# One decoder layer on one core: the router of each token tile inside the next tile's output projection, the sample tile kept by halves on 128 partitions, the router's logits in four column strips

## The chip, the core and the metric

The kernel runs on one core of a Trainium2 chip. The metric is the device time of one execution in microseconds (us). A smaller number is better.

## What is computed

One layer of a hybrid decoder for 256 prompt tokens and 64 sample tokens (8 sequences of 8), all in fp32. Attention, a gated linear recurrence and their merge come first; none of that is touched. What follows is this:

```python
h = x + merged @ w_o                                   # (320, 1024) @ (1024, 1024)
x2 = rmsnorm(h, norm2)
logits = x2 @ w_router + b_router                      # 32 experts
top_v, top_e = lax.top_k(logits, 4); gate = softmax(top_v)
# every expert: its tokens, in slots
u = x @ w1[e] + b1[e]                                  # (1024 -> 2048), glu and lin interleaved
y = (min(glu,7) * sigmoid(1.702*glu) * (clip(lin)+1)) @ w2[e] + b2[e]
out = h + sum over the 4 experts of gate * y
```

The weights of the 32 experts are 12 MB each (8 for w1, 4 for w2), 384 MB together, and each is read once.

## The kernel before, in words

The tokens are three tiles (`TILES`): 128 and 128 prompt tokens, and 64 sample tokens. Each engine has its program written out by hand, and semaphores tie them together; there is no planner, so the order of the work is the order of the calls in each engine's block.

**The weight stream.** Expert weights pass through `ring`, 19 slots of 1 MB. `CHUNKS` (L88) is their order: w1 of an expert in 8 chunks, w2 in 4, with the w2 of an expert after the w1 of the next in part. The SP queue issues chunks 0 to 6 once two state outputs have left, 7 and 8 in the first branch projection, 9 to 14 when the merge is done, and 15 to 18 when the output projection of all three tiles is done (`sp.wait_ge(h_psum, 3)`, L388), because they go where `w_o` lay. From chunk 19 on, each waits until the chunk that had its slot 19 places earlier has been used (`await_used`, L372).

**The stage around the change.** TensorE (PE) runs this list, L850 to L866:

```python
project_h(0); project_h(1); turn_h(0); project_h(2); turn_h(1)
logits(0); turn_h(2); logits(1); logits(2)
for t in range(3): places(t)
```

`project_h` (L799) is one tile's output projection: 32 matmuls of 128x512 in two column halves for a prompt tile (L810), and for the sample tile 32 of 64x512 whose halves run side by side on column tiles (L815). `turn_h` (L819) transposes h, 8 times 128x128. `logits` (L831) multiplies the transposed h by the router's weights, 8 steps of k into one 32-column result. `places` (L841) counts with triangular and all-one matrices which slot a token has at each expert. An fp32 matmul of the code is two instructions in the trace. VectorE (DVE) does `add_h` (h = x + projection, L1576), `turned_h` (copies the transposed h out of PSUM and multiplies by norm2, L1588), `rms_h` (L1596), then `choose` for the three tiles (L1603: bias, top 8, indices, one-hot, sum, the last two being L1608 to L1618), one `placed` (L1639), and `pick_tokens` (L1673), six compares that build the 0/1 matrices `pick` of the first two experts. ScalarE (ACT) does `squares_h` and `root_h` (L1213, L1220): the sum of squares, the root, and `hn`, the normed h. The sample tile lies on partitions 0 to 63 with all 1024 columns.

Then the experts run in pairs, `body(p)` (L983). `gather` (L880) multiplies `pick` by `hn`, six matmuls of 512 columns (L886, 12 instructions), of which two have 64 rows; ACT copies the result (L1268), PE transposes it (L895), DVE multiplies it by norm2. `up` (L899, L914) is w1 of an expert, 64 instructions, `down` (L951) is w2, 32; L928 turns u; `combine` (L968) adds y to `acc` with DVE's `add` (L1726). The gather of the next pair is the last work of each body; only the first stands before the bodies. `last_body` (L1017) has another order: its second `up` waits for DVE's adds of the pair before. At the end `store_tile` (L419) writes the three tiles of `acc`.

## Time and profile before

| what | value |
|---|---|
| median of 3 runs | 1259.48 us (1259.46 to 1260.38) |
| the profiled execution, its own time | 1260.13 us |
| its span in the trace | 1258.3 us |
| busy: PE, DVE, ACT | 1204.7, 346.0, 185.8 us |
| moved by DMA | 439.83 MB, mean 350 GB/s |
| mean granted clock of TensorE | 0.991 |

The profiled execution took 0.65 us more than the median; the span lacks 1.8 us of it, before the first and after the last record. "PE" rows are matmuls, "PEld" rows weight loads, "SPq" the issue of transfers. In a row of the timeline, the second number is the time from the start of the group to its end, and a bracket says how long the engine was idle before it and what ended that. In a row of the windows, the numbers are the stretch, its length, and the busy time of PE, PEld, DVE, ACT and POOL with their instructions, then the granted clock (1 is full), the DMA share and GB/s. Matmuls overlap, so the distance between the starts of two groups tells more than the length of one.

### The profile page before, as it was taken

The page shows a single profiled execution, that of the slowest core. Times are in us where ns is not written, and L with a number is a line of the kernel's source. Part 1 is how long each engine was busy: PE and PEld are TensorE (multiplying, and loading weights), DVE is VectorE, ACT ScalarE, POOL GpSimd, SP SyncE. Part 2 cuts the span into 40 slices and gives each one's busy share as a digit, 9 for nine tenths or more (in the row PEclk, how much of TensorE's full clock was granted, in tenths as well). Part 3 has the DMA queues.
Part 4 walks back from the last instruction along what each step waited for, and adds up shares of the span by engine and source line. Part 5 has one row for each costly group of instructions (what it writes and reads, how often), then busy time and mean ns, then how long its engine had stood idle before and what let it go on. Part 6 is the DMA issues. An engine that isn't in the chain of part 4 may idle for free.

```text
span 1258.3 us, 12744 instructions
## 1 busy us (share of the span) xinstructions
PE 1204.7 (96%) x5349; PEld 542.6 (43%) x5349; DVE 346.0 (27%) x727; ACT 185.8 (15%) x330; POOL 24.9 (2%) x49
## 2 busy tenths in 40 slices
PE   5999999998999999999999999999999999999987
PEld 4776678744333434343333434333333333333332
DVE  2405423614232222223132222321221313131222
ACT  2115321003111111111011111111010101010111
POOL 4101000000000000000000000000000000000000
PEclk9999998998999999999999999999999999999999
DMA  9833153943999999999999999999999999999995
GB/s 242 261 114 120 34 134 119 393 203 134 375 381 418 417 417 417 418 418 416 417 418 416 417 419 416 416 418 417 417 418 417 416 417 417 417 417 417 417 416 213
DMA packets 101484, 439.83 MB, mean 350 GB/s; under 512 B 15822, under 2 KB 31536, under 8 KB 68608
## 3 DMA queue, kind: packets, MB, share of 16 engines
q1 hardware_dynamic: 99632, 434.88, 86.8%
q0 software_dynamic: 1776, 4.09, 1.1%
q8 instruction: 44, 0.72, 0.2%
q14 instruction: 16, 0.13, 0.0%
q10 hardware_dynamic: 16, 0.00, 0.0%
HBM read 436.26 MB, written 3.67 MB: 350 GB/s over the span
## 4 chain that ended last, share of the span: by engine, by line
PE 74%; DMA 17%; SPq 4%; ACT 2%; DVE 1%; issue 1%; DVEq 0%; ACTq 0%
PE ps L914 25%; DMA ring<-in_w 17%; PE ps L951 13%; PE ps L581 10%; PE ps L886 7%; PE ps L968 5%; PE ps L783 3%; PE ps L810 2%; SPq L370 2%; SPq L368 2%; PE ps L928 1%; PE ps L559 1%; PE ps L895 1%; ACT xnT L1258 1%; DMA acc<-in_x_sample 1%
## 5 line engine op out<-in xcount | busy, mean ns | idle before, releaser
L914 PE MATMUL ps<-ring,hnT 128*64 128x512 f32 x2048 | 451.8, 595 | 14.7 <-DMA ring<-in_w 11.3
L914 PEld LDWEIGHTS ps<-ring,hnT 128*64 128x64 f32 x2048 | 155.4, 137 | 298.3 <-issue 262.4
L951 PE MATMUL ps<-ring,xnT 128*64 128x512 f32 x1024 | 230.6, 598 | 5.0 <-DMA ring<-in_w 3.6
L951 PEld LDWEIGHTS ps<-ring,xnT 128*64 128x64 f32 x1024 | 78.0, 138 | 150.8 <-issue 130.5
L1708 DVE TENSOR_TENSOR xnT<-ps,b1T 128x512 f32<-128x512 f32 x32 | 22.1, 692 | 415.8 <-PE ps L928 415.8
L581 PE MATMUL ps<-xnT,ring 128*128 128x320 f32 x464 | 130.3, 436 | 0.6 <-DVE xnT L1343 0.6
L1729 DVE TENSOR_TENSOR acc<-acc,ps 128x1024 f32<-128x1024 f32 x34 | 41.4, 1218 | 235.6 <-PE ps L968 235.6
L1245 ACT COPY hnT<-ps 128x1024 f32<-128x1024 f32 x32 | 32.4, 1012 | 481.1 <-PE ps L914 481.1
L581 PEld LDWEIGHTS ps<-xnT,ring 128*128 128x128 f32 x464 | 86.5, 190 | 37.8 <-issue 2.2
L886 PE MATMUL ps<-region,cst 128*128 128x512 f32 (+1 forms) x192 | 97.7, 635 | 1.6 <-DVE cst L1678 1.6
L968 PE MATMUL ps<-xnT,cst 128*128 128x512 f32 (+1 forms) x192 | 79.1, 617 | 4.2 <-ACT xnT L1258 2.7
L886 PEld LDWEIGHTS ps<-region,cst 128*128 128x128 f32 (+1 forms) x192 | 31.6, 190 | 55.7 <-issue 54.6
L1257 ACT COPY xnT<-ps 64x512 f32<-64x512 f32 x32 | 18.5, 579 | 239.9 <-PE ps L951 239.9
L968 PEld LDWEIGHTS ps<-xnT,cst 128*128 128x128 f32 (+1 forms) x192 | 25.0, 171 | 48.4 <-issue 42.1
L928 PEld LDWEIGHTS ps<-cst,hnT 128*128 128x128 f32 x256 | 33.2, 209 | 28.3 <-issue 23.5
L928 PE MATMUL ps<-cst,hnT 128*128 128x128 f32 x256 | 39.2, 296 | 2.8 <-ACT hnT L1245 2.8
L1700 DVE TENSOR_TENSOR hnT<-ps,cols 128x512 f32<-128x512 f32 x32 | 21.9, 692 | 58.7 <-PE ps L895 58.6
L1268 ACT COPY hnT<-ps 128x512 f32<-128x512 f32 x32 | 18.7, 585 | 69.0 <-PE ps L886 69.0
L810 PE MATMUL ps<-ring,xnT 128*128 128x512 f32 x64 | 27.7, 593 | 1.2 <-issue 1.2
L1251 ACT ACTIVATE sig<-xnT 128x512 f32<-128x512 f32 x32 | 20.2, 630 | 27.4 <-DVE xnT L1712 27.4
L1688 DVE TENSOR_SCALAR cst<-cst,place,gates 128x64 f32<-128x64 f32 (+1 forms) x96 | 22.6, 303 | 0.0
L1719 DVE SCALAR_TENSOR_TENSOR hnT<-hnT,xnT 128x512 f32<-128x512 f32 x32 | 22.2, 693 | 1.1
(255 smaller groups left out, 668.5 us busy)
## 6 DMA issues: line engine op xcount, KB each, us to landing
ring<-in_w SPq DMA_DIRECT2D x384, 1024.0 KB, 22.1
ring<-in_w_in SPq DMA_DIRECT2D x15, 1024.0 KB, 5.7
ring<-in_w_o SPq DMA_DIRECT2D x1, 4096.0 KB, 16.3
acc<-in_x_prompt SPq DMA_DIRECT2D x4, 512.0 KB, 9.4
ring<-in_w_in SPq DMA_DIRECT2D x8, 256.0 KB, 5.8
ring<-in_w_a SPq DMA_DIRECT2D x2, 1024.0 KB, 10.2
ring<-in_w_b SPq DMA_DIRECT2D x1, 2048.0 KB, 15.4
out<-ring POOLq DMA_DIRECT2D x1, 1024.0 KB, 7.9
```

The source lines that it names most:

```text
L368: sp.dma_start(ring[:, m, :], w1v[e, k]).then_inc(chunk_in[m], 16)
L370: sp.dma_start(ring[:, m, :].rearrange("p (f c) -> p f c", f=2), w2v[e, k]).then_inc(chunk_in[m], 16)
L581: mm = pe.matmul(ps[:, bank, 0:T], unit(m)[:, k, c:c + P], xnT[:, k, :], start=(k == 0), stop=(k == KD - 1))
L783: mm = pe.matmul(ps[:, u % 3, 0:T], w_sb[:, k, P * m:P * m + P], operand[:, k, :], start=(k == 0), stop=(k == 3))
L810: mm = pe.matmul(ps[:, (XB, VB_)[t] + c, :], xnT[:, k, t0:t0 + r], wo_sb[:, k, 512 * c:512 * c + 512], start=(k == 0), stop=(k == KD - 1))
L886: mm = pe.matmul(ps[:, XB + half, :], pick[0:r, t, :], hn[0:r, t, 512 * half:512 * half + 512], start=(t == 0), stop=(t == 2))
L914: mm = pe.matmul(ps[o:o + 64, q // 2, :], xeT[:, k, SLOTS * which:SLOTS * (which + 1)], ring[:, slot, 512 * q:512 * q + 512], start=(k == ...
L928: mm = pe.transpose(ps[:, 2 + gl, o:o + P], u_sb[:, q, 256 * r + gl:256 * r + gl + 255:2], ident)
L951: mm = pe.matmul(ps[64 * c:64 * c + 64, 6, :], hT[:, which, order_of(f), :], ring[:, slot, D * (f % 2) + 512 * c:D * (f % 2) + 512 * c + 512],
L968: mm = pe.matmul(out, lhsT, rhs[:, 512 * half:512 * half + 512], start=True, stop=True)
L1245: nc.scalar.copy(u_sb[:, :, :], ps[:, 0:2, :]).then_inc(u_copied, 1)
L1729: dve.tensor_tensor(acc[:, t, :], acc[:, t, :], ps[:, bank:bank + 2, :].rearrange("p a b -> p (a b)"), ALU.add).then_inc(comb_added, 1)
```

## The change

Three things. (1) PE's list is cut up: the second half of tile 1's projection and all of tile 2's are issued in pieces, and between the pieces stand the transposes, logits and places of the tile before. DVE and ACT are put in the same order, tile by tile, and each tile's `pick` for the first two experts is made as soon as its places are known, so that the first gather's parts for tiles 0 and 1 run before tile 2's choice. (2) Logits come in four column strips: the router's weights, scaled once by norm2 on DVE, become the 32-column stationary operand, four k at a time side by side, two steps; ACT copies the 128-partition result, and one matmul with a constant `fold` adds the strips and turns the result. (3) The sample tile lies by halves on 128 partitions: columns 0 to 511 on partitions 0 to 63, columns 512 to 1023 on 64 to 127, in `acc`, `hn`, loads, stores and adds. Its sum of squares is joined over the two halves by a matmul with the constant `twin`, its transposes are four, and the 64-row matmuls of every gather lie on different row halves, next to each other. `pick_tokens` is three instead of six operations. The constants grow by 224 columns.

```diff
@@ constants
-                  ("chunk_of", 4), ("seq_of", 8), ("head_of", 4), ("keep", 320), ("slot", 128),
-                  ("expert", 32)]:
+                  ("chunk_of", 4), ("seq_of", 8), ("head_of", 4), ("keep", 320), ("slot", 64),
+                  ("expert", 32), ("twin", 128), ("before_s", 128), ("fold", 32)]:
@@ SP: loads and stores of the sample tile
+            for half in range(2):
+                sp.dma_start(acc[64 * half:64 * half + 64, 2, 0:512], x_half(x_sample, half)
+                             ).then_inc(x_again[2], 16)
...
+                    for half in range(2):
+                        sp.dma_start(x_half(y_sample, half), acc[64 * half:64 * half + 64, 2, 0:512]).then_inc(y_out, 16)
@@ PE: new functions
+            def logit_parts(t):
+                t0, r = TILES[t]
+                pe.wait_ge(hnT_ready, t + 1)
...
+                for step in range(2):
+                    for a in range(4):
+                        k = 4 * step + a
+                        mm = pe.matmul(ps[32 * a:32 * a + 32, 2, 0:r], w_rt[:, k, :], hnT[:, k, t0:t0 + r],
+                                       start=(step == 0), stop=(step == 1))
+                mm.then_inc(lgp_psum, 1)
+
+            def logits(t):
+                pe.wait_ge(lgp_copied, t + 1)
...
+                pe.matmul(ps[:, 0, 0:EXPERTS], lg_parts, const("fold"), start=True, stop=True).then_inc(lg_psum, 1)
...
+            def twin_sum():
+                pe.wait_ge(ss2_ready, 3)
+                pe.wait_ge(placed_freed, 1)
+                pe.matmul(ps[:, NB, 128:129], const("twin"), small[:, 46:47], start=True, stop=True).then_inc(twin_psum, 1)
+
+            def pick_part(half, t, start, stop):
+                if t < 2:
+                    return pe.matmul(ps[:, XB + half, :], pick[:, t, :], hn[:, t, 512 * half:512 * half + 512],
+                                     start=start, stop=stop, skip_group_check=True)
+                return pe.matmul(ps[:, XB + half, :], pick[64 * half:64 * half + 64, 2, :],
+                                 hn[64 * half:64 * half + 64, 2, 0:512], start=start, stop=stop, skip_group_check=True)
+
+            def first_part(half, t):
+                pe.wait_ge(pick_ready, t + 1)
+                pe.wait_ge(hn_ready, t + 1)
...
+                pick_part(half, t, start=(t == 0), stop=False)
@@ PE: the order
-            project_h(0)
-            project_h(1)
+            project_h(0, 0, range(KD))
+            project_h(0, 1, range(KD), last=True)
+            project_h(1, 0, range(KD))
             turn_h(0)
-            project_h(2)
+            project_h(1, 1, range(4))
+            logit_parts(0)
+            project_h(1, 1, range(4, 6))
+            logits(0)
+            project_h(1, 1, range(6, KD), last=True)
+            pe.wait_ge(pads_ready, 6)
+            project_h(2, 0, range(2))
+            places(0, [0])
             turn_h(1)
-            logits(0)
+            project_h(2, 0, range(2, 4))
+            logit_parts(1)
+            project_h(2, 0, range(4, 5))
+            logits(1)
+            project_h(2, 0, range(5, KD), last=True)
+            places(1, [0, 1])
             turn_h(2)
-            logits(1)
+            first_part(0, 0)
+            twin_sum()
+            logit_parts(2)
+            first_part(1, 0)
             logits(2)
...
+            first_part(0, 1)
+            first_part(1, 1)
+            places(2, [0, 1])
+            places(2, [2])
+            pe.wait_ge(pick_ready, 3)
+            pe.wait_ge(hn_ready, 3)
+            for half in range(2):
+                pick_part(half, 2, start=False, stop=True).then_inc(gather_done, 1)
@@ PE: every later gather
                 for half in range(2):
-                    for t, (_, r) in enumerate(TILES):
-                        mm = pe.matmul(ps[:, XB + half, :], pick[0:r, t, :], hn[0:r, t, 512 * half:512 * half + 512],
-                                       start=(t == 0), stop=(t == 2))
-                    mm.then_inc(gather_done, 1)
+                    pick_part(half, 2, start=True, stop=False)
+                for half in range(2):
+                    pick_part(half, 0, start=False, stop=False)
+                    pick_part(half, 1, start=False, stop=True).then_inc(gather_done, 1)
@@ ACT: order
+            squares_h(0)
+            root_h(0)
+            copy_parts(0)
+            squares_h(1)
+            root_h(1)
+            copy_parts(1)
+            squares_h(2)
+            act.wait_ge(hnT_psum, 3)
+            nc.scalar.copy(hnT[:, :, PROMPT:T].rearrange("p (h k) s -> p k h s", h=2),
+                           ps[:, 0, :].rearrange("p (k h s) -> p k h s", k=4, h=2)).then_inc(hnT_ready, 1)
+            copy_parts(2)
+            root_h(2)
@@ DVE: order
             add_h(0)
+            rms_h(0)
+            dve.tensor_tensor(w_rt[:, :, :], w_rt[:, :, :], wide(cols[:, 8:16].unsqueeze(2), [P, KD, EXPERTS]), ALU.mult
+                              ).then_inc(rt_scaled, 1)
             dve.wait_ge(stores, 16 * 20)
             turned_h(0)
-            rms_h(0)
+            choose(0)
             add_h(1)
+            placed(0)
+            turned_h(1)
             rms_h(1)
+            choose(1)
             add_h(2)
-            turned_h(1)
-            turned_h(2)
+            placed(1)
             rms_h(2)
-            for t in range(3):
-                choose(t)
-            placed()
+            choose(2)
+            placed(2)
```

`placed(t)` is one operation as before plus one compare of 128x128 for `pick`; `copy_parts(t)` is ACT's copy of the strips, 128x128 (two of 128x64 for tile 2). `weigh`, which works out the gate weights after the first gather, has six operations in place of twelve. The six matmuls that count the tokens of each expert stand between the last part of the first gather and its transposes.

## Rows read from the trace of the kernel before

**Rows 1.** The page: transfer rate in 40 slices; the chain by line.
```profile
GB/s 242 261 114 120 34 134 119 393 203 134 375 381 418 417 417 417 418 418 416 417 418 416 417 419 416 416 418 417 417 418 417 416 417 417 417 417 417 417 416 213
...
PE ps L914 25%; DMA ring<-in_w 17%; PE ps L951 13%; PE ps L581 10%; PE ps L886 7%; PE ps L968 5%; PE ps L783 3%; PE ps L810 2%; SPq L370 2%; SPq L368 2%; PE ps L928 1%; PE ps L559 1%; PE ps L895 1%; ACT xnT L1258 1%; DMA acc<-in_x_sample 1%
```

**Rows 2.** Windows: busy us (x instructions) of engines, PEclk, DMA share, GB/s.
```profile
304.00:306.00 2.00, 1.44 (x2) 0.83 (x3) 0.41 (x3) 0.00 (x0) 0.00 (x0) 0.50 0.00 0
...
368.00:370.00 2.00, 2.00 (x12) 0.86 (x10) 1.19 (x7) 0.00 (x0) 0.00 (x0) 1.00 0.55 86
370.00:375.00 5.00, 5.00 (x26) 1.98 (x24) 0.00 (x0) 0.00 (x0) 0.00 (x0) 1.00 0.85 331
...
1242.00:1244.00 2.00, 2.00 (x12) 0.75 (x10) 0.00 (x0) 0.00 (x0) 0.00 (x0) 1.00 0.12 47
```

**Rows 3.** Timeline of PE in later bodies: start, us, line [idle before].
```profile
593.27 13.95 PE L914 MATMUL ps<-ring,hnT 128*64 128x512 f32 x64 [0.16 <-issue]
...
650.01 13.95 PE L914 MATMUL ps<-ring,hnT 128*64 128x512 f32 x64 [0.16 <-issue]
...
1155.41 1.94 PE L914 MATMUL ps<-ring,hnT 128*64 128x512 f32 x8 [0.22 <-DMA ring<-in_w]
```

**Rows 4.** Chain of waits, gather to first expert: start us, us, what.
```profile
304.56 7.68 PE ps L886 x12
...
312.90 0.65 PE ps L895 x4
...
313.60 13.98 PE ps L914 x64
```

**Rows 5.** Timeline of the stage, PE and the weight queue.
```profile
255.20 27.70 PE L810 MATMUL ps<-ring,xnT 128*128 128x512 f32 x64 [1.15 <-issue]
...
282.75 1.04 PE L827 MATMUL ps<-cst,acc 128*128 128x128 f32 x8
...
283.71 7.09 PE L815 MATMUL ps<-ring,xnT 128*64 128x512 f32 x32
...
291.21 24.73 SPq L370 DMA_DIRECT2D ring<-in_w  x4
```

**Rows 6.** Timeline of VectorE: first and last operation of a choice, compares.
```profile
295.06 0.25 DVE L1608 SCALAR_TENSOR_TENSOR xnT<-ps,small,b_rt 128x32 f32<-128x32 f32 x1
...
296.41 0.37 DVE L1616 TENSOR_REDUCE sel<-xnT 128x32 f32<-128x128 f32 x1
...
303.35 1.06 DVE L1678 TENSOR_SCALAR cst<-cst,place 128x64 f32<-128x64 f32 x6
```

**Rows 7.** Chain in attention: column strips, row halves, plain projection.
```profile
69.44 1.22 PE ps L573 x16
...
124.12 1.06 PE ps L619 x8
125.19 4.50 PE ps L581 x16
```

**Rows 8.** Timeline of PE's weight loads inside one body's gather.
```profile
1178.53 0.29 PEld L886 LDWEIGHTS ps<-region,cst 64*128 64x128 f32 x2 [0.76 <-issue]
1179.58 0.30 PEld L886 LDWEIGHTS ps<-region,cst 128*128 128x128 f32 x2 [0.76 <-issue]
```

**Rows 9.** Windows where the granted clock is below full.
```profile
350.00:355.00 5.00, 5.00 (x21) 1.52 (x19) 0.14 (x1) 0.00 (x0) 0.00 (x0) 0.77 1.03 428
...
294.40:297.80 3.40, 1.94 (x16) 1.86 (x16) 2.56 (x13) 2.58 (x3) 0.00 (x0) 0.99 1.00 400
...
304.60:308.00 3.40, 3.40 (x4) 1.10 (x4) 0.00 (x0) 0.00 (x0) 0.00 (x0) 0.50 0.00 0
```

**Rows 10.** Timeline of the last 50 us: tile 2's add, last matmuls, stores.
```profile
1214.24 0.69 DVE L1733 TENSOR_TENSOR acc<-acc,ps 64x512 f32<-64x512 f32 x1
...
1239.62 7.09 PE L951 MATMUL ps<-ring,xnT 128*64 128x512 f32 x32 [1.32 <-issue]
...
1251.41 3.56 SPq L422 DMA_DIRECT2D out<-acc  x3
```

271 lines of the change are left out of this document (140 added, 131 removed).

## The prediction

> **What bounds the kernel now.** I read the page first. In slices 13 to 39 of its 40 the transfers run at 416 to 419 GB/s, and the chain that ended last holds both PE lines and the weight transfer with 17% [rows 1]. So two things share the bound, and the question is where each does. A pair of experts is 24 chunks of 1.0486 MB; at 417 GB/s a chunk takes 2.51 us and a pair 60.3. PE's own period, where nothing waits for DMA, is 650.01 - 593.27 = 56.7 us [rows 3]. PE is thus faster by 3.6 us a pair, lives on the ring's 19 slots for some bodies, and then stands behind the stream: late bodies wait before single chunks [rows 3]. From there on the end is set by when the stream started, not by what PE does in the middle.
>
> When did it start? The windows show the transfers at rest before the first expert, and once more short of full between 368 and 375 us [rows 2]: there 2 x 0.45 + 5 x 0.15 = 1.7 us are missing by share, 2.6 by GB/s. This is the place that decides. The first body uses 20 chunks, 20 are loaded behind it, and the 21st place comes free only with the first chunk of the second body's first matmuls. After 375 the stream never pauses. So **the time at which the second body begins passes to the end one to one**: whatever PE saves before it is kept, whatever PE saves in the bodies after it is lost in the wait for chunks, until the last stretch, where the stream is over before PE is (its share is 0.12 in 1242 to 1244 [rows 2], while the last `down` runs to 1246.7 and the stores start at 1251.41 [rows 10]).
>
> Ahead of the second body lies the stage that the change rebuilds. PE is dense from 255.20 to 290.8: projections of tiles 0 and 1 in 27.7 us, transposes of tile 0, tile 2's projection in 7.09 [rows 5]. Then come 14 us of transposes, logits, choices and places, most of it waiting for DVE, and from 304.56 the gather, 7.68 us, and the copy and the transposes, to the first expert at 313.60 [rows 4].
>
> **Part by part, the stage.** Prices: an instruction of 128x512 takes 27.7/64 = 0.433 us, eight transposes 1.04 [rows 5]. Four column strips appear in the attention part: 16 instructions of 320 columns take 1.22 [rows 7]; by columns 128 would be 0.49, and 16 weight loads bound it below, so I take 0.6 (0.4 for 64 columns), with 0.49 and 1.22 as ends. A change of the tile shape on PE costs something: two 64-row instructions between others span 1179.58 - 1178.53 = 1.05 us, not 0.87, so 0.2 with the exposed weight load [rows 8].
>
> A rule of the Trainium skill speaks against the change here: its page "TensorEngine Tiling (Array Packing)", section "Key Properties", says that switching the tiling mode, not just the tile, drains TensorE. By the row the drain is 0.2 us, and the sum goes by that.
>
> Until tile 2's projection is done, PE gets, in front of the 290.8 of before: tile 1's transposes 1.0, two sets of strips 1.2, two folding matmuls 0.5, tile 0's places 0.25 and nine shape changes 1.8. That is 4.8, so it ends at 295.6. The choices run beside it. A choice takes 296.41 + 0.37 - 295.06 = 1.7 us on DVE up to `sel` [rows 6]; tile 0's starts near 283.5 and `sel` is there at 285.3, where PE wants it at 287.4; tile 1's transposes need DVE's add by 287.6 and get it at 286.7; tile 1's second set of strips waits for DVE's copy until 290.0, and PE comes at 290.6; tile 1's fold needs ACT's copy at 292.3 and PE comes at 292.6. All are in time, the last two by half a microsecond: if that cover goes, each late item adds its lateness. The add of tile 1 on DVE now queues behind `choose(0)`, the copy of the strips on ACT behind `root_h`; both are in these times.
>
> After 295.6: DVE's add of tile 2 0.7 (one operation of 128x512 in place of two), four transposes 0.5, the first `pick` piece 0.87, the `twin` matmul 0.25, strips with shape changes 0.8, a piece 0.87, the fold 0.25: 299.8, with 0.3 for handovers 300.1. Then the only serial piece left, tile 2's choice: `sel` 1.75 later, 301.9. In its shadow PE runs two pieces, 1.73, and the places of tiles 0 and 1, 0.5, to 302.4; the last place matmul, 302.7; DVE's `placed` and one compare, 0.3 + 0.35 (two of the compares of 1.06/6 [rows 6]) with handovers 0.1: 303.5. Four 64-row pieces remain of the gather. They lie on different row halves; eight such instructions of 256 columns took 1.06 us, where plain ones of 320 columns take 4.50/16 = 0.28 each, or 0.225 at 256 and 1.80 for eight [rows 7]. The first pass of the second half can run beside the second pass of the first: 4 become 3 steps, 1.3 us, bounded by 0.87 and 1.73. With a shape change: 305.0. Six counting matmuls 0.5 + 0.2, the eight transposes 1.06 + 0.2: **the first expert at 307.0 instead of 313.6, 6.6 us earlier.** ACT's exponentials lie between its last `hn` and the gather's copies, as before, under the choice and the places.
>
> **Clock.** The granted clock fell to 0.50, the lower level of 1.2 GHz, after 294.4 to 297.8, in which PE had 1.94 us of 32-column logits, and was still there in 304.6 to 308.0, where four gather instructions took 3.4 us [rows 9], twice their price. That loss of 1.7 us is inside the old 313.6 and not in my 307.0, which is at full clock. The new stage is denser, but 301 to 306 holds waits; I charge 0.6 for a fall there, between 0 and 3. The dip in 350 to 355 (0.77, 1.2 us lost) behind the narrow bias matmuls of the first body I take to stay.
>
> **Handovers.** The new chain has a dozen more semaphores on the edge of PE's order; I charge 0.6.
>
> **The first body.** Its gather for the next pair has 12 instructions with four shape changes, 5.2 + 0.8; the new order has 1.3 + 8 x 0.433 + two changes = 5.2: 0.8 saved, ahead of the second body, so kept. In the 13 bodies after it the same 0.8 is worth nothing (cover: the stream, 60.3 against now 55.9). If the stream were not the bound, it would be 10 us more.
>
> **The last stretch.** Gather of the last pair 0.8, and the adds of tile 2 before the last `up`, one operation less, 0.7 [rows 10]. Together 1.5, and the stream allows it: the last chunks land before 1244 and the last `down` wants its fourth near 1239.6 + 5.3 = 1244.9 [rows 2, 10]. Below nothing it can't be, above 1.5 the chunks stop it. At the very end one add less, 0.7, against one more transfer to issue; three took 3.56 us with their waits for DVE [rows 10]; I take 0.3 for it: 0.4 left.
>
> **At nothing:** 112 KB more constants, 0.3 us of transfer among the first projections (cover: PE's L581, which the chain holds there [rows 1]; without it, 0.3), the second load of x by one more issue on SP, first needed by the add at 269, chunks 15 to 18 issued 5 us later than at 291.21 [rows 5]: 10 us of transfer, done near 306, wanted in the second `up` after 321. SP has nothing else queued behind that wait but chunk 19, which waits for the first expert. `weigh`, the scaling of the router's weights and `pick_tokens` lie under PE's matmuls.
>
> **Sum:** 6.6 - 0.6 - 0.6 + 0.8 + 1.5 + 0.4 = 8.1 us off. The profiled execution took 1260.13, so 1252.0; against the median of 1259.48, 1251.4.
>
> **Rivals.**
> *A, as above:* 0.62, own range 1249.3 to 1253.5. The low side is strips at 0.49, no fall of the clock, and no dip near 350.
> *B, the clock falls under the first expert.* The stretch before it is now small matmuls, a wait for the last choice, and transposes. If the lower level, which before lay over some 10 us, from 297.8 at the earliest to 308.0 [rows 9], lies over 303 to 313, the first `up` runs at half speed in it: 6 us at half the clock do 3 us of work, and with the small things ahead of it 3.6 more are lost than A holds. For: the fall came behind just such matmuls. Against: gather pieces now stand among them. 1255.0; chance 0.17.
> *C, handovers stall PE.* The two covers of about half a microsecond fail and each of the waits behind (strips, fold, choice) is late by as much again: 2 us, 1253.6; 0.11. Against: where the old chain changes engines, from ACT's copy to 312.90 and on to 313.60, it leaves less than 0.1 us [rows 4].
> *D, the stream does not move.* If the pause at 368 to 375 were not PE's doing but the stream's own, the end would stay but for 1 us at the very end: 1258.5. For: 17% of the chain is the transfer. Against: with every slot loaded there is nothing to send, and at 304 to 306 the share is 0 [rows 2]. 0.04.
> *E, slower: the shape changes.* The old stage had PE pass 35 us without a break; the new one cuts in strips, halves and full shapes, some 16 changes to the first expert. I price each at 0.2. At 0.7 the gain is eaten, at 0.9 the kernel takes 1262.5. That is the skill's rule with a large price. The 0.18 of [rows 8] speaks against; but it was seen between 64 rows and 128 only, not between 32 columns and 128. 0.04.
> The remaining 0.02 is that the change doesn't save because the strips don't run side by side: then 3 x 1.1 us more, 1254.7, still faster.
>
> **The numbers.** A measurement here tells 0.2% or 2.5 us from nothing. Faster: A, B, C and the rest, less a little for B beyond bounds, 0.91; same: D, 0.05; slower: E, 0.04. The range has to take A whole, C, and B's middle: 1249.0 to 1255.4.
>
> **What would show it.** First L914 of the first expert (`up`) near 307 to 308 where it was 313.60; tile 2's projection ending near 296; DVE's three choices at about 283.5, 293 and 300; the strips 0.6 us a set; the last two `pick` pieces within 1.3; a gather of 5.1 in every body; the pause near 361 to 367 still there; PE's idle time before chunks larger than now by about 0.8 a body. Wrong would be: transfers without that pause, PE waits of over half a microsecond between projection pieces, or 0.50 as the clock under the first `up`.

## The result, and the profile after

The changed kernel takes 1245.79 us (median of 9 runs, 1243.53 to 1251.26); the kernel before, run beside it, 1259.46 (9 runs, 1253.59 to 1263.27). The ratio is 0.9899, with a 95% interval of 0.9879 to 0.9920: faster by 1.0%. The forecast was 1251.4, in a range of 1249.0 to 1255.4. The sign was right; the gain was 13.7 us and not 8.1, outside the range. One run of `after_third` (2457.11 us) and one of `late_bias_fill` (1551.94) further on were slow ones: the medians in the table below contain them, the ratios leave them out.

The profiled execution took 1247.42 us with a span of 1245.6, 12.7 less than before. PE is busy for 1181.6 us (1204.7 before), DVE for 327.6 (346.0), ACT for 186.0, and the mean granted clock is 0.996 (0.991). Lines of the code have moved; those of the rows below are: L823 and L828 output projection (prompt, sample tile), L841 transposes of h, L855 strips, L863 fold, L876 places, L885 `twin`, L889 and L891 gather with 128 and 64 rows, L938 counts, L968 transposes after the gather, L987 `up`, L1001 transposes of u, L1024 `down`, L1041 `combine`; on DVE L1677 the add of tile 2, L1700 to L1710 a choice, L1716 and L1719 `placed` and the compare, L1789 the multiplication by norm2.

The page of the kernel after: transfer rate in 40 slices, and the chain by line.

```profile
GB/s 263 243 81 150 44 135 39 401 281 167 417 416 417 417 416 418 417 417 416 418 417 417 418 418 417 417 417 416 418 417 416 417 417 416 417 417 417 417 417 229
...
DMA ring<-in_w 26%; PE ps L987 21%; PE ps L596 10%; PE ps L1024 9%; SPq L381 4%; PE ps L1041 4%; PE ps L889 4%; SPq L383 3%; PE ps L798 3%; PE ps L823 2%; PE ps L1001 1%; PE ps L574 1%; PE ps L891 1%; PE ps L968 1%; PE ps L715 1%
```

Against [rows 1]: full rate from the eleventh slice on, with none below it until the last, where before the eleventh and twelfth held 375 and 381. The transfer is now 26% of the chain in place of 17%.

The windows of the kernel after, where before had no transfers and then a pause [rows 2], and where its clock was down [rows 9]; columns as in front.

```profile
294.40:297.80 3.40, 3.17 (x33) 1.92 (x29) 1.35 (x5) 1.30 (x3) 0.00 (x0) 1.00 0.46 125
297.80:301.20 3.40, 3.40 (x16) 1.93 (x13) 1.65 (x9) 3.25 (x11) 0.00 (x0) 1.00 0.99 405
301.20:304.60 3.40, 2.48 (x18) 1.34 (x19) 0.48 (x2) 1.21 (x4) 0.00 (x0) 1.00 1.02 418
304.60:308.00 3.40, 3.10 (x18) 1.15 (x19) 3.25 (x11) 0.00 (x0) 0.00 (x0) 1.00 0.73 290
360.00:362.00 2.00, 2.00 (x12) 0.86 (x10) 0.00 (x0) 0.00 (x0) 0.00 (x0) 1.00 0.97 391
...
368.00:370.00 2.00, 2.00 (x12) 0.81 (x10) 0.00 (x0) 1.01 (x1) 0.00 (x0) 1.00 1.04 416
370.00:375.00 5.00, 5.00 (x26) 1.95 (x24) 0.00 (x0) 0.00 (x0) 0.00 (x0) 1.00 1.02 418
350.00:355.00 5.00, 4.76 (x18) 2.35 (x19) 2.96 (x6) 1.55 (x3) 0.00 (x0) 1.00 1.01 418
```

Two things that the prediction took for given are gone: the clock is at its full level (2.4 GHz) in every one of these stretches, and the pause of the stream behind the first body doesn't come, which the prediction had named as a sign of being wrong.

The chain of waits of the kernel after, from tile 2's first matmuls to the first expert (start us, us, what). "x4" with 0.7 us is half of eight instructions where the other half hides.

```profile
285.40 1.87 PE ps L828 x8
287.27 0.34 PE ps L876 x2
287.61 0.91 PE ps L841 x8
288.52 1.87 PE ps L828 x8
290.38 0.57 PE ps L855 x16
290.96 1.01 PE ps L828 x4
291.97 0.34 PE ps L863 x2
292.31 2.75 PE ps L828 x12
...
295.08 0.70 DVE acc L1677
...
297.45 0.36 PE ps L855 x16
...
301.55 0.20 DVE place L1716
...
301.77 0.30 DVE cst L1719
...
302.12 1.18 PE ps L891 x4
303.30 0.57 ACT hnT L1362
...
303.92 0.67 PE ps L968 x4
...
304.61 0.70 DVE hnT L1789
...
305.36 0.64 PE ps L987
```

In this execution the projection starts at 255.83 (255.20 before [rows 5]), so this list has to be read 0.63 earlier against the old one. The first expert starts at 305.36 in place of 313.60 [rows 4]: from the projection's start that is **49.53 us in place of 58.40**. No piece of the projection waits for another engine; the strips take 0.57 a set and 0.36 for tile 2, and the only waits of PE above 0.1 us are DVE's add, the last choice's end (`placed` and the compare), and behind the gather ACT's copy and DVE's multiplication.

PE's groups in the first body, before (313.60 to 366.31) and after (305.36 to 354.83); columns: count, busy us and mean ns, idle.

```profile
L951 PE MATMUL ps<-ring,xnT 128*64 128x512 f32 x32 | 8.8, 712 | 0.0
L886 PE MATMUL ps<-region,cst 128*128 128x512 f32 (+1 forms) x12 | 6.0, 626 | 0.0
```
```profile
L1024 PE MATMUL ps<-ring,xnT 128*64 128x512 f32 x32 | 7.1, 595 | 0.0
L889 PE MATMUL ps<-region,cst 128*128 128x512 f32 x8 | 3.7, 606 | 0.0
L891 PE MATMUL ps<-region,cst 64*128 64x512 f32 x4 | 1.2, 629 | 0.0
```

The first body lost 3.2 us, 52.71 to 49.47: `down` 1.7 because the fall of the clock is gone (0.77 in 350 to 355 before [rows 9], 1.00 now), the gather 1.3. And from the timeline of PE at the end of the kernel after, the last chunk's matmuls:

```profile
1226.19 5.50 PE L1024 MATMUL ps<-ring,xnT 128*64 128x512 f32 x24 [1.32 <-ACT xnT L1352]
1232.24 1.94 PE L1024 MATMUL ps<-ring,xnT 128*64 128x512 f32 x8 [0.55 <-DMA ring<-in_w]
```

The last `down` starts 13.4 us earlier than at 1239.62 [rows 10], and its fourth part then stands 0.55 us for the last chunk.

So the 12.7 us of span are: projection 0.63 later, stage 8.87 shorter, first body 3.24 shorter, all that follows the second body's start 1.2 shorter (892.0 to 890.8).

### The profile page after: what moved, and what is told of

Read it like the earlier page. It is cut to its first block, busy times and chain, and to the rows that moved or that the text cites. A ratio compares the mean times of both kernels' runs of the same rounds, so it can differ in the third digit from the quotient of the medians.

```text
span 1245.6 us, 12704 instructions
## 1 busy us (share of the span) xinstructions
PE 1181.6 (95%) x5353; PEld 529.7 (43%) x5353; DVE 327.6 (26%) x656; ACT 186.0 (15%) x335; POOL 24.9 (2%) x49
## 4 chain that ended last, share of the span: by engine, by line
PE 62%; DMA 26%; SPq 7%; ACT 2%; DVE 1%; issue 1%; DVEq 0%; ACTq 0%
DMA ring<-in_w 26%; PE ps L987 21%; PE ps L596 10%; PE ps L1024 9%; SPq L381 4%; PE ps L1041 4%; PE ps L889 4%; SPq L383 3%; PE ps L798 3%; PE ps L823 2%; PE ps L1001 1%; PE ps L574 1%; PE ps L891 1%; PE ps L968 1%; PE ps L715 1%
## 5 line engine op out<-in xcount | busy, mean ns | idle before, releaser
L987 PE MATMUL ps<-ring,hnT 128*64 128x512 f32 x2048 | 453.7, 595 | 15.6 <-DMA ring<-in_w 14.9
L987 PEld LDWEIGHTS ps<-ring,hnT 128*64 128x64 f32 x2048 | 154.4, 137 | 302.0 <-issue 253.0
L1024 PE MATMUL ps<-ring,xnT 128*64 128x512 f32 x1024 | 233.1, 596 | 16.1 <-DMA ring<-in_w 14.7
L1024 PEld LDWEIGHTS ps<-ring,xnT 128*64 128x64 f32 x1024 | 73.7, 137 | 169.1 <-issue 122.0
L596 PE MATMUL ps<-xnT,ring 128*128 128x320 f32 x464 | 134.2, 446 | 0.5 <-DVE xnT L1437 0.5
L1041 PE MATMUL ps<-xnT,cst 128*128 128x512 f32 (+1 forms) x192 | 79.1, 617 | 4.3 <-ACT xnT L1352 2.7
L889 PE MATMUL ps<-region,cst 128*128 128x512 f32 x128 | 59.6, 606 | 0.0
L1041 PEld LDWEIGHTS ps<-xnT,cst 128*128 128x128 f32 (+1 forms) x192 | 25.0, 171 | 48.5 <-issue 42.1
L1001 PEld LDWEIGHTS ps<-cst,hnT 128*128 128x128 f32 x256 | 33.1, 208 | 28.3 <-issue 23.5
L1001 PE MATMUL ps<-cst,hnT 128*128 128x128 f32 x256 | 39.2, 296 | 2.8 <-ACT hnT L1339 2.8
L889 PEld LDWEIGHTS ps<-region,cst 128*128 128x128 f32 x128 | 22.8, 189 | 33.5 <-issue 33.4
L1789 DVE TENSOR_TENSOR hnT<-ps,cols 128x512 f32<-128x512 f32 x32 | 22.0, 691 | 31.7 <-PE ps L968 29.7
L823 PE MATMUL ps<-ring,xnT 128*128 128x512 f32 x64 | 28.4, 596 | 1.2 <-issue 1.2
L1362 ACT COPY hnT<-ps 128x512 f32<-128x512 f32 x32 | 18.6, 585 | 40.4 <-PE ps L889 38.5
L968 PE MATMUL ps<-cst,hnT 128*128 128x128 f32 x128 | 20.0, 280 | 3.9 <-ACT hnT L1362 3.9
```

The costliest lines, as they stand in the source:

```text
L596: mm = pe.matmul(ps[:, bank, 0:T], unit(m)[:, k, c:c + P], xnT[:, k, :], start=(k == 0), stop=(k == KD - 1))
L823: mm = pe.matmul(ps[:, (XB, VB_)[t] + c, :], xnT[:, k, t0:t0 + r], wo_sb[:, k, 512 * c:512 * c + 512], start=(k == 0), stop=(k == KD - 1), ...
L889: return pe.matmul(ps[:, XB + half, :], pick[:, t, :], hn[:, t, 512 * half:512 * half + 512], start=start, stop=stop, skip_group_check=True)
L968: mm = pe.transpose(ps[:, bank, P * k:P * k + P], xe[:, P * (4 * half + k):P * (4 * half + k) + P], ident)
L987: mm = pe.matmul(ps[o:o + 64, q // 2, :], xeT[:, k, SLOTS * which:SLOTS * (which + 1)], ring[:, slot, 512 * q:512 * q + 512], start=(k == ...
L1001: mm = pe.transpose(ps[:, 2 + gl, o:o + P], u_sb[:, q, 256 * r + gl:256 * r + gl + 255:2], ident)
```

## The experiments

Each edit is to the kernel after, unless it says before. `fill(n)` is n matmuls of 128x512 whose result is thrown away, 2 x 0.433 us each; they are the price of PE time at a place. In the text "stage" is from the projection's start to the first `up`, "first body" from there to the next body's first `up`, "rest" from there to the end of the span; "median" has the ratio to before with its interval. The profiled executions gave:

| kernel | stage | first body | rest | median | ratio |
|---|---|---|---|---|---|
| before | 58.40 | 52.71 | 892.0 | 1259.46 | |
| after | 49.53 | 49.47 | 890.8 | 1245.79 | 0.9899 (0.9879 to 0.9920) |
| after_again | 49.53 | 49.47 | 891.2 | 1246.29 | 0.9904 (0.9881 to 0.9927) |
| after_third | 49.52 | 49.47 | 890.6 | 1244.19 | 0.9881 (0.9846 to 0.9917) |
| fill_first | 54.35 | 51.16 | 891.3 | 1252.01 | 0.9940 (0.9916 to 0.9963) |
| fill_body0 | 49.53 | 54.63 | 890.7 | 1248.77 | 0.9930 (0.9904 to 0.9955) |
| fill_body5 | 49.53 | 49.47 | 891.3 | 1244.28 | 0.9891 (0.9867 to 0.9914) |
| uncut | 60.12 | 49.48 | 891.2 | 1254.92 | 0.9957 (0.9939 to 0.9975) |
| uncut_filled | 56.61 | 49.47 | 891.4 | 1250.95 | 0.9948 (0.9929 to 0.9968) |
| late_gather | 54.00 | 49.47 | 890.7 | 1246.59 | 0.9887 (0.9860 to 0.9913) |
| late_gather_filled | 52.25 | 51.12 | 891.5 | 1248.05 | 0.9912 (0.9879 to 0.9944) |
| plain_logits | 51.16 | 51.17 | 892.2 | 1248.99 | 0.9913 (0.9886 to 0.9940) |
| before_filled | 55.96 | 51.02 | 892.0 | 1252.69 | 0.9938 (0.9914 to 0.9963) |
| old_gather_mid | 49.53 | 49.47 | 891.6 | 1242.72 | 0.9876 (0.9851 to 0.9900) |
| old_gather_ends | 49.80 | 53.61 | 891.8 | 1245.74 | 0.9897 (0.9873 to 0.9920) |
| warm | 49.53 | 51.17 | 890.7 | 1247.47 | 0.9915 (0.9892 to 0.9939) |
| late_bias | 49.53 | 45.30 | 895.4 | 1244.62 | 0.9880 (0.9847 to 0.9914) |
| late_bias_fill | 49.53 | 50.46 | 891.5 | 1244.94 | 0.9888 (0.9852 to 0.9925) |

**Where a microsecond of PE counts.** Unchanged kernel, then the same 5.2 us of throwaway matmuls put in three places.

```diff
 # fill_first: before the first expert; fill_body0: in body 0; fill_body5: in body 5
+            def fill(n):
+                for _ in range(n):
+                    pe.matmul(ps[:, 1, :], ident, cst[:, 0:512], start=True, stop=True)
...
+                        fill(6)                      # fill_first
...
+                if main and p == 0: fill(6)          # fill_body0
+                if main and p == 5: fill(6)          # fill_body5
```

> The changed kernel again, as the control for the three kernels beside it. All theories: 0.987 to 0.992 of the kernel before. If the spread of the times comes from where the granted clock falls, its slower runs are those with the lower mean clock: about 1.2 us for each 0.001 of mean clock below 0.999 at most (0.001 of 1245 us is 2.5 us at half the clock).

> Six more 128x512 matmuls (12 instructions, 12 x 0.43 = 5.2 us) on PE between the first gather and its transposes; their result is thrown away. Theory S (the end is the first use of a chunk plus the stream of 365 chunks): first expert 5.2 us later less what of the copies they cover (0.5), and the end 4.5 to 5.2 us later than the changed kernel, 0.9935 to 0.994 of before. Theory P (every us of PE work counts, wherever it is): the same. A theory in which the transfers alone set the end: under 1 us.

> The same 5.2 us of matmuls in the first body, before its gather for the second pair. Theory S: in the changed kernel the transfers have no rest near 357 us, since 20 chunks from the first use at 307.2 run to 357.6 and the place for the 21st is free at 356.8; the filler makes that rest come back, so 5.2 less about 1: the end 3.5 to 4.7 us later than the changed kernel. Theory P: 5.2 later. If nothing after the first expert counts: 0.

> The same 5.2 us of matmuls in the sixth body. Theory S: PE has gained 60.3 - 55.2 = 5 us a body on the stream and stands behind it, so the end does not move (within 1 us of the changed kernel), and PE's waits for chunks are 5 us shorter in total. Theory P: 5.2 us later.

Measured against after_again (1246.29, same chip): before the first expert +5.7, in body 0 +2.5, in body 5 -2.0. In the profiles fill_first has 4.8 more in the stage, and a fall of the clock adds 1.7 in the first body. fill_body0 has 5.1 more from first expert to end (945.3 against 940.2; 940.7 and 940.0 in the other two profiles of the kernel after), and its rest, 890.7, is as in the kernel after. fill_body5 has 940.7 from the first expert to the end: nothing. The windows of fill_body0 show the pause again:

```profile
356.00:358.00 2.00, 2.00 (x6) 0.77 (x5) 0.00 (x0) 0.59 (x1) 0.00 (x0) 1.00 1.02 422
358.00:360.00 2.00, 1.76 (x13) 1.06 (x13) 1.22 (x2) 0.59 (x1) 0.00 (x0) 1.00 0.58 242
360.00:362.00 2.00, 2.00 (x12) 0.75 (x10) 2.00 (x10) 0.00 (x0) 0.00 (x0) 1.00 0.07 25
362.00:364.00 2.00, 2.00 (x12) 0.86 (x10) 0.10 (x1) 0.00 (x0) 0.00 (x0) 1.00 0.58 176
```

By share (0.42 + 0.93 + 0.42) x 2 = 3.5 us of transfer are missing, by rate against 417 GB/s 3.9; the last microsecond of the 5.1 I can't place in the windows. So the step on which the prediction stood holds in the profiles: time added before the second body counts in full, time in body 5 not at all. The median of fill_body0 shows only half of it (2.5 of 5.1); its runs lie between 1245.16 and 1253.11, and the section on the chip says why medians of six or seven are that rough.

**How much is overlap, how much is clock.** uncut issues tile 1's and tile 2's projections in one piece, as the old list did, and changes nothing on DVE and ACT, whose order stays the one made for the interleaved list; late_gather puts the first gather's parts behind the last places; plain_logits computes the logits of tiles 0 and 1 the old way, in eight steps into one 32-column result. before_filled is the kernel before, with five throwaway matmuls where PE waits anyway.

```diff
 # uncut
             turn_h(0)
-            project_h(1, 1, range(4))
+            project_h(1, 1, range(KD), last=True)
+            pe.wait_ge(pads_ready, 6)
+            project_h(2, 0, range(KD), last=True)
             logit_parts(0)
...
 # late_gather
-            first_part(0, 0)
             twin_sum()
...
             places(2, [2])
+            first_part(0, 0); first_part(1, 0); first_part(0, 1); first_part(1, 1)
...
 # plain_logits, t < 2
+                    for k in range(KD):
+                        mm = pe.matmul(ps[:, 0, 0:EXPERTS], hnT[:, k, t0:t0 + r], w_rt[:, k, :],
+                                       start=(k == 0), stop=(k == KD - 1))
...
 # before_filled, to the kernel before
             logits(0)
             turn_h(2)
+            fill(1)
             logits(1)
+            fill(1)
             logits(2)
             for t in range(3):
                 places(t)
+                if t == 1: fill(1)
...
+            fill(2)
```

> The changed kernel with the projections of tiles 1 and 2 run whole, and the strips, folds, places and transposes of tiles 0 and 1 behind them; strips, halves and early gather parts stay. Stage length (start of tile 0's projection to first expert matmul) is 58.4 us before and 49.5 changed. Theory 1 (the interleaving is the larger part of the gain): two choices of 1.7 us, tile 1's add and transposes and the strips come out of cover: stage 55 to 57 us, the end 5 to 8 us later than the changed kernel. Theory 2 (the shorter gather and the strips are it): stage under 52 us, end within 2.5.

> The changed kernel with the four gather parts of tiles 0 and 1 moved behind tile 2's choice and places. Their 8 x 0.43 = 3.5 us come out of cover, and PE waits during the choice instead: stage 52.5 to 53.5 us, end 3 to 4 us later than the changed kernel, if the clock stays. Rival: the clock falls in the thinner stretch, as before the change, and the first expert starts at half the clock: 5 to 8 us later.

> The changed kernel with the logits of tiles 0 and 1 as before (8 steps of k, 16 instructions in 1.9 us in place of 0.6 for the strips, 0.14 to 0.34 for the fold, and two shape changes); tile 2 keeps the strips. Theory 1 (PE's own list sets the stage): 2 x (1.9 - 0.9) = 2 us longer stage, end 1.5 to 2 later. Rival (the strips are hidden by DVE's choices and change nothing): stage within 0.5 us.

> The kernel before, with five 128x512 matmuls of fp32 (0.87 us each) into an unused PSUM bank where PE waits in the router stage: behind tile 2's transposes, between the logits, behind tile 1's places, and two before the gather. Results thrown away. Theory C (a part of the gain is the clock that no longer falls in the router): the granted clock stays at 1 to the first expert, the gather takes 5.9 us in place of 7.7, and the kernel is 1 to 3 us faster than before (0.9975 to 0.999) though it does more. Rival (the clock has no share): 0 to 1 us slower.

uncut loses 10.6 us of stage and is slower there than the kernel before (60.12 against 58.40). Its windows say that this is not waiting alone:

```profile
290.00:300.00 10.00, 5.69 (x46) 3.31 (x46) 4.57 (x14) 1.54 (x4) 0.00 (x0) 0.80 0.71 260
300.00:310.00 10.00, 7.86 (x50) 4.99 (x43) 3.00 (x13) 4.38 (x11) 0.00 (x0) 0.51 0.40 160
310.00:315.00 5.00, 4.16 (x23) 2.09 (x21) 2.09 (x10) 2.36 (x9) 0.00 (x0) 1.00 0.02 3
```

PE waits 4.3 of 10 us, and then is at the lower level, 1.2 GHz. late_gather has the same in small (0.70 in 290 to 300) and loses 4.5 us of stage in its profile; its median, 1246.59, doesn't show them, and here profile and medians stay apart. plain_logits loses 1.6 us of stage for two tiles, and its clock falls once in the first body. **before_filled is the clearest run**: it computes just what the kernel before does, with 4.3 us of PE work more, and is faster by 0.6% (0.9938, 0.9914 to 0.9963). The windows of before_filled, to be set against [rows 9], and PE's timeline of it:

```profile
290.00:300.00 10.00, 9.73 (x65) 6.07 (x64) 6.96 (x35) 3.81 (x9) 0.00 (x0) 1.00 0.87 355
300.00:305.00 5.00, 5.00 (x12) 1.77 (x11) 0.00 (x0) 0.59 (x1) 0.00 (x0) 1.00 0.01 3
```
```profile
299.97 5.90 PE L895 MATMUL ps<-region,cst 128*128 128x512 f32 x12
...
307.24 4.94 PE L923 MATMUL ps<-ring,hnT 128*64 128x512 f32 x22
```

The same twelve gather instructions take 5.9 us here and took 7.68 [rows 4]. In the profiles that is 2.4 us of stage and 1.7 of first body, 4.1 together. Only the 2.4 lie where the fills stand; the fall in the first body comes in some executions of the same code and not in others (last section), so one profile can't say that the fills took it away. The medians of that set differ by 7.1 (1259.75 to 1252.69), and the profiled before_filled began its projection 3.9 earlier, through unchanged work: a fall behind the 16-column matmuls of the gated recurrence (L721), which the profile of the kernel before has, is missing there. The two windows, the kernel before first:

```profile
210.00:220.00 10.00, 10.00 (x48) 8.39 (x48) 1.85 (x2) 3.11 (x5) 0.00 (x0) 0.66 0.98 349
210.00:220.00 10.00, 10.00 (x56) 8.10 (x56) 4.09 (x5) 2.99 (x4) 0.00 (x0) 1.00 1.01 367
```

How much of the 7.1 beyond 2.4 the fills brought stays open.

The next two set the clock right and leave the order wrong, which parts the two gains, as far as the fills don't take time themselves.

```diff
 # uncut_filled: uncut, and where the pieces of the projection stood
             logit_parts(0)
             logits(0)
+            fill(2)
             places(0, [0])
+            fill(1)
             turn_h(1)
+            fill(1)
             logit_parts(1)
+            fill(1)
             logits(1)
+            fill(2)
...
 # late_gather_filled: late_gather, and where the gather's parts stood
+            fill(1)
             twin_sum()
             logit_parts(2)
+            fill(1)
             logits(2)
             places(2, [0, 1])
+            fill(1)
             places(2, [2])
```

> The kernel with the projections run whole and the router of tiles 0 and 1 behind them, as in the run called uncut, and seven 128x512 matmuls (0.87 us each, result thrown away) where PE waited in it. It tells apart what the interleaving gives by cover and what by the clock: uncut had 13.7 us at the lower level around its router and a stage of 60.1 us. If the clock is half of it: the level stays at 1, stage 55.5 to 57 us, 1250 to 1252 us or 0.993 of before, 3 us faster than uncut although it does more. If cover is all: stage 59 to 61, no faster than uncut.

> The kernel of late_gather (first gather parts behind tile 2's choice) with three 128x512 matmuls (0.87 us each, thrown away) where PE waited. It holds the clock at its upper level, so that the stage shows what the cover alone is worth: 51.5 to 53 us against 49.5, where late_gather had 54.0 with 6.8 us at the lower level. If the rest of the stage's growth was cover alone: 54.

uncut_filled's stage is 56.6 at a clock of 0.999: of uncut's 10.6 us, at least 3.5 are clock and at most 7.1 are cover that is lost. Part of the 7.1 is DVE's order: in uncut's chain the add of tile 1 starts at 295.17, right behind `choose(0)`, though tile 1's projection is long done. And 56.61 is no better than before_filled's 55.96: without the interleaving, the strips and the early gather parts gain the stage nothing. late_gather_filled needs 52.25: 2.7 for the gather's cover, and the rest of late_gather's 4.5 is clock. At full clock, the interleaving of the projection with the engine order that goes with it is the largest part of the change, the gather's place the second (2.7, from one profile each), the strips the third (1.6 with two of three tiles). These are prices of taking one part out of the finished kernel. They don't add up: together 11.4, where the whole stage gained 6.4 at full clock (55.96 to 49.53).

**The gather.** Its old order (three tiles per half, the 64-row parts apart) back in the middle bodies alone, or in the first and the last gather inside a body alone.

```diff
+                if gates_copied is not None and isinstance(p, int) and 2 <= p <= 14:   # ends: p in (1, 15)
+                    for half in range(2):
+                        pick_part(half, 0, start=True, stop=False)
+                        pick_part(half, 1, start=False, stop=False)
+                        pick_part(half, 2, start=False, stop=True).then_inc(gather_done, 1)
...
```

> The changed kernel with the old order of the six matmuls (64-row piece last in each half) in the gathers for pairs 2 to 14, that is in bodies 1 to 13: 13 x 1.3 = 17 us more PE work, all of it behind the second body. Theory S (the end follows the start of the second body, PE gains 5 us a body on the stream): the same time as the changed kernel within 1 us, 0.989 to 0.991 of before, and PE's waits for chunks 17 us shorter. Theory P (all PE work counts): 17 us slower, 1.003 of before.

> The changed kernel with that old order only in the gathers for pairs 1 and 15, in the first body and ahead of the last pair: 1.35 us each. Theory S: the second body begins 1.35 us later and the end follows; the last one is partly under the stream. First body 50.8 us in place of 49.5, end 1.3 to 2.2 us later than the changed kernel, measured from the start of the first expert: 941.6 to 942.5 in place of 940.3. Rival (the first body has 1 us of slack on the stream): 940.3 to 941.

In the middle it costs nothing: 1242.72, nominally the fastest kernel of all, ratio 0.9876 (0.9851 to 0.9900), which the kernel after's interval overlaps. PE's groups from 420 us on, of old_gather_mid and of the kernel after, show where the slower gather goes:

```profile
L994 PE MATMUL ps<-ring,hnT 128*64 128x512 f32 x1738 | 384.5, 595 | 13.6 <-DMA ring<-in_w 11.4 <-issue 1.8 <-DVE acc L1828 0.3
L1031 PE MATMUL ps<-ring,xnT 128*64 128x512 f32 x928 | 208.3, 594 | 6.1 <-DMA ring<-in_w 4.5 <-ACT xnT L1359 1.3
L889 PE MATMUL ps<-region,cst 128*128 128x512 f32 x104 | 51.3, 617 | 0.0
L891 PE MATMUL ps<-region,cst 64*128 64x512 f32 x52 | 28.1, 640 | 0.0
```
```profile
L987 PE MATMUL ps<-ring,hnT 128*64 128x512 f32 x1748 | 388.4, 595 | 15.3 <-DMA ring<-in_w 14.9 <-DVE acc L1821 0.3
L1024 PE MATMUL ps<-ring,xnT 128*64 128x512 f32 x928 | 211.9, 596 | 16.1 <-DMA ring<-in_w 14.7 <-ACT xnT L1352 1.3
L889 PE MATMUL ps<-region,cst 128*128 128x512 f32 x104 | 48.1, 605 | 0.0
L891 PE MATMUL ps<-region,cst 64*128 64x512 f32 x52 | 15.3, 629 | 0.0
```

13 gathers take 16 us more (51.3 + 28.1 against 48.1 + 15.3), and the waits for chunks are 13.7 less (15.9 against 29.6). The four 64-row instructions on different row halves take 1.18 us for four in the kernel after; 52 of them 15.3. old_gather_ends was meant to show 1.3 us at each end; its profiled execution had two falls of the clock in the first body (53.61), its median none of the cost: inconclusive. One of the falls bears on the prediction, since the stage of this kernel is that of the kernel after; the first `up` and a window just behind its start:

```profile
303.71 14.90 PE L994 MATMUL ps<-ring,hnT 128*64 128x512 f32 x64
304.00:306.00 2.00, 2.00 (x6) 0.48 (x5) 1.90 (x7) 0.00 (x0) 0.00 (x0) 0.58 0.49 190
```

The lower level lies under the start of the first expert, which is the prediction's rival B in small: the stage took 0.27 more and the first `up` 14.90 in place of 13.95.

**Can the falls be prevented ahead of the stage?** A throwaway matmul in the middle of the narrow transposes of `b1`, one in the sample tile's attention, and the first piece of the first branch moved between the two narrow outputs of the gated recurrence for the sample tile.

```diff
+                    if gl:
+                        pe.matmul(ps[:, WB, 0:256], ident, cst[:, 0:256], start=True, stop=True)
...
+                    if s == 4 and g:
+                        pe.wait_ge(pj_freed, FIRST_RB + 12)
+                        pe.matmul(ps[:, (FIRST_RB + 14) % 3, :], ident, cst[:, 0:512], start=True, stop=True)
...
-                19: [lambda: gla_out(True)],
+                19: [lambda: gla_out(True, first_branch)],
```

> The changed kernel with the narrow stretches ahead of the output projection broken up: the first branch matmuls moved between the two halves of the sample tile's 16-column matmuls, one 128x512 matmul (0.87 us) in the middle of the sample tile's attention, and one of 256 columns (0.43) in the middle of the 32x32 transposes. Theory C (what differs from run to run is where the clock falls in the narrow stretches of the attention part, 1.7 us for each 3.4 at the lower level, 0 to 4 times): most runs at mean clock 0.999, median 1242.5 to 1245 and a narrower spread than the changed kernel's 7.7 us. Rival (the falls come anyway): 1 us slower than the changed kernel.

A miss: 1247.47, and the clock still fell, right behind the transposes that the first new matmul breaks up (0.88 in 50 to 60) and in the first body (0.95 in 330 to 340, 0.88 in 340 to 350). The spread narrowed, 1245.72 to 1249.48, but six runs are no proof of that.

**Is more to be had before the second body?** The matmuls that add the second bias of the experts, weighted by the gates (L1041 with `b2r`, three times 1.4 us in the first body), move into body 4, where PE's time is free; late_bias_fill puts the 5.2 us of throwaway matmuls into body 0 besides.

```diff
-                    add_biases(0, XB)
+                    token(XB)                        # one column, keeps the count of the semaphore
...
+                combine_ = combine_biased if main and p == 4 else combine
```

> The changed kernel once more, as the control on the chip of these three: 0.987 to 0.992 of before, stage 49.5, first expert's start to end 940.2 to 940.8 if the clock does not fall in the first body, 1.7 more if it does.

> The changed kernel with the twelve bias matmuls (5.0 us of PE) and their adds taken out of the first body and accumulated in the combines of the fifth, where the stream is ahead of PE's need; the first body keeps three one-column matmuls for the order. Theory S (after the change the stream runs without a rest from the first use on, so that only the first use counts and the first body has slack below its 49.5 us): first body 44.5 to 45 us, but from the first expert's start to the end 939.3 to 940.3 us, against 940.3 to 940.8 of the changed kernel: 0 to 1 us faster, 0.988 to 0.99 of before. Theory P1 (PE time in the first body counts one to one downwards too): 935.5, 5 us faster, 0.986.

> The kernel of late_bias with the 5.2 us of thrown-away matmuls in the first body. Theory S: the slack takes the filler up; first expert's start to the end 940 to 941 us, where the same filler in the changed kernel made 945.3. Theory P1: 5 us more than late_bias.

late_bias shortens the first body to 45.30 and gains nothing: the rest grows to 895.4, and from the first expert to the end it is 940.7, as in the three profiles of the kernel after (940.2, 940.7, 940.0). With the fill the body is 50.46 and the total 942.0: of 5.2 us more, 1.3 reach the end. **So there are two bounds.** As long as the first body takes more than some 49.4 us, the end is the second body's start + 891; below that the stream, which goes on without a pause once the first expert frees its first slot, is the bound, and the end is the first expert's start + 940.5. The kernel after has 49.47, just at the corner. The lower bound rests on late_bias and its filled twin, one profile each, and both sums hold to about 1 us: the rest lies between 890.6 and 892.2 in the profiles with a first body above 49.4.

## Why the prediction was right or wrong

*What bounds it, and where a microsecond counts.* Right, and shown. fill_first, fill_body0 and fill_body5 give 4.8 in the stage and 1.7 of clock behind it, 5.1, and nothing in the profiles. But "whatever PE saves before it is kept" holds only down to 49.4 us of first body; late_bias shows the end of it. I had said that the pause near 361 to 367 would still be there; it is gone, since the body's 49.5 us are about what 20 chunks take (20 x 2.51 = 50.2). Here this cost the forecast nothing that can be seen; had the change saved 2 us more in the first body, they would have been lost.

*The stage, 5.4 predicted net, 8.87 measured.* Three steps failed, all the same way.
- "A change of the tile shape on PE costs something ... 0.2" and "nine shape changes 1.8". Tile 2's projection ends 39.2 us behind the projection's start (295.06 - 255.83), where I had 40.4. By the chain a set of strips takes 0.57, not 0.6 + 0.2, a fold 0.14 to 0.34, places 0.34. The old list took 35.6 to this point; of the 3.6 us more, tile 1's transposes (0.91), two sets of strips, two folds and the places are 2.9, which leaves some 0.8 for nine changes: under 0.1 each, where I charged 0.2. The rule of the Trainium skill ("TensorEngine Tiling (Array Packing)", "Key Properties"), that a switch of mode drains TensorE, may well be so, and no run here tests it by itself; its price in this trace is below what I charged. Rival E, which made the rule large, found no support.
- From there to the first expert: 11.4 by my sum (307.0 - 295.6), 10.3 measured. The way from the projection's end to tile 2's fold took 3.95 and not 4.5, because strips and `twin` cost 0.48 where I had 1.05; the last places and DVE's `placed` took 1.31 in place of 1.6; the 64-row pieces took 1.18, against 1.3 and a shape change. Behind them the sum came out by luck: I had 2.0 us of PE's own work there, counting matmuls and transposes, and forgot ACT's copy and DVE's multiplication. By the chain it is 0.57 for the copy, 0.67 for half of the transposes and 0.70 for the multiplication, 2.06 with handovers, with the counting matmuls (303.18) in the shadow of the copy (303.30).
- "I charge 0.6 for a fall there" and "Handovers ... I charge 0.6": neither came. The choices ran on DVE at 283.64, 292.34 and 299.05, all in time, and the half-microsecond covers held.

*The clock.* It was priced by less than half. The loss inside the old stage was in the sum, since the new one was added up at full clock (1.7 us were named, before_filled shows 2.4); "The dip in 350 to 355 ... I take to stay" was the wrong step, 1.7 us. Its place was read rightly, behind the 32-row bias matmuls, but I took one execution's fall for a property of the code: the same bias matmuls stand in the kernel after, at 337.37, and the clock behind them is 1.00. In four other profiled executions the fall does come, and each time it takes the same 1.7 us. before_filled, whose edit adds work and changes no order, has none of these falls and shows what they cost the profiled execution of the kernel before: 4.1 us, a third of the 12.7 between the two profiles. The 1.7 in the first body may be the luck of these executions, and the change can't be credited with it; the stage's part can be, for nine profiled executions with its order have a stage of 49.5 us. Why a fall comes in one execution and not in the next is open; warm, with its own fills, had one.

*The gather, "5.2 + 0.8 ... the new order ... 5.2: 0.8 saved".* It took 5.93 before (358.82 to 364.75) and 4.64 after (348.69 to 353.33): 1.3 saved. I had 1.3 for the four 64-row instructions and 0.2 for each of two changes; the four take 1.11 with the first change in it, and the eight others 3.53, 0.07 above 8 x 0.433, which is all that is left of the second. In the later bodies it is worth nothing, as said: old_gather_mid.

*The last stretch and the very end, 1.9 predicted, 1.2 measured.* The rest fell from 892.0 to 890.8 (891.2 and 890.6 in the other two profiles of the kernel after). Up to the start of the last `down` 1.95 us were saved, more than the 1.5 of the sum. "The stream allows it" was too generous: the last chunk comes 0.55 us late for the last `down`, and from its start to the last `combine` the kernel after takes 0.9 longer. Behind that 0.2 were saved, where I had 0.4.

*The sum.* 8.1 against 12.7 in the profile: stage +3.5, first body +2.4, end -0.7, and -0.6 for a projection that happened to begin 0.63 later. That start isn't the change's: unchanged work precedes it, and it moves from run to run with the falls of the clock in it (last section). So the failed terms are sizes: the shape changes, the strips, the handovers and the charge for a fall in the stage, which were too dear, and the fall in the first body, which was taken to stay. The mechanism, work before the second body counted one to one, held.

*The range and the rivals.* A was the case, but its own low side, 1249.3, had "no fall of the clock, and no dip near 350" with strips at 0.49, and it still kept the nine changes, the handovers and the gather's price at my values. These were upper bounds taken as middles. C, D and E didn't happen. B didn't happen in the profiled execution of the result; old_gather_ends, with the same stage, shows it in small (0.58 under the first `up`, 1.2 us), so it was a matter of chance and smaller than priced. In uncut, one edit away, the lower level lies over 10 us (0.51 in 300 to 310), but ahead of the first expert, which starts at 316.52.

## What to carry to other kernels

Find the one place where a stream that bounds the kernel stands idle: only work ahead of it counts, and only until the pause is closed; 5 us of PE time were worth 5 us in the first body and nothing in the sixth. When serial work is woven between dense matmuls, count the clock as a gain of its own, and test it cheaply: put throwaway matmuls where the engine waits, with which the kernel before here ran 0.6% faster, although only 2.4 us of it can be traced to the place of the fills. Bounds that lean to one side (shape changes, handovers, charges for falls) should be added as bounds and not as middles, or five small cautions become one wrong forecast.

## What the chip did that was not expected

**The same kernel spreads by some 10 us, and the clock goes with it.** The kernel before ran 16 times beside before_filled, between 1255.38 us at a mean granted clock of 0.994 and 1266.64 at 0.984; the kernel after between 1243.5 and 1251.3. 0.001 of mean clock is about 1.1 us (11.3 us over 0.010) in the kernel before. In the kernel after the two go together less closely: its slowest run has the lowest clock (1251.26 at 0.992), but runs at 0.996 lie between 1243.8 and 1247.8. None of the 57 runs of the kernel before beside the experiments has a mean clock above 0.994, while the kernel after reached 0.999. That fits with falls in the old stage in every one of them, but only one of them has a profile. Six runs of before_filled, at 0.997 to 1.000, spread by 3.7 us.

**Falls come and go in unchanged work.** Identical instructions ahead of the stage let the projection start anywhere from 249.5 to 256.4 us in the profiled executions. The seven that have no stretch of 10 us below a clock of 0.99 ahead of it start between 249.5 and 251.7, the eleven that have one (near 50, 170 or 215 us) between 252.4 and 256.4. And the first body, the same code, took 49.47 or 49.48 us in eight of them and 51.12 to 51.17 in four. PE was busy throughout in both. In the four, as in the kernel before, the 1.7 us are lost at the lower level directly behind 32-row bias matmuls, behind the first four of them in late_gather_filled and behind the last eight in the others. The windows of plain_logits, whose bias matmuls run from 332.70 to 335.62:

```profile
334.00:336.00 2.00, 2.00 (x8) 0.39 (x8) 1.28 (x2) 0.00 (x0) 0.00 (x0) 0.96 1.03 410
336.00:338.00 2.00, 2.00 (x6) 0.49 (x4) 0.54 (x1) 0.00 (x0) 0.00 (x0) 0.50 1.04 418
338.00:340.00 2.00, 2.00 (x10) 0.69 (x8) 0.00 (x0) 0.00 (x0) 0.00 (x0) 0.68 1.05 438
```

In 336 to 338 PE gets six instructions where it otherwise shows twelve, and the transfers go on at full rate. The two kernels without these matmuls in the first body, late_bias and late_bias_fill, showed no fall there. The Trainium skill ("TensorE: Matmul & The Clock Gate", "Part 1: The HAM clock gate") says that the number of slow matmuls at a kernel's start varies from run to run; the runs here show falls that vary from run to run far behind the start as well, near 170 and 215 us, in the stage and in the first body; between 360 and 1225 us none of the 18 profiled executions has one (mean clock 1.00).

**Neighbouring 64-row matmuls overlap more than their passes suggest.** Four instructions of 512 columns on two row halves take 1.11 to 1.18 us next to each other, where four plain ones take 4 x 0.433 = 1.73 and four 64-row ones in the old order 28.1/13 = 2.2.
